# Experts loaded in an order made on the chip, one quad with two blocks of slots per weight load, and residual norms per token tile

## The chip, the cores and the metric

The kernel runs on one core of one Trainium2 chip. The metric is device time in microseconds (us), from one launch to its end. In a core, TensorE (PE in the profile; PEld is its weight load) multiplies, VectorE (DVE), ScalarE (ACT) and GpSimd (POOL) do elementwise work, and SyncE (SP) here only starts transfers. They meet at semaphores. SBUF is the on-chip memory; PSUM, 8 banks of 128 x 512 float32, takes TensorE's results. All data are float32.

## The reference

Two transformer-like blocks on 256 tokens of 1024 channels. The first has attention, a mixture of experts, a pooling mixer, and a second mixture of experts. The second has a mixer, a feed-forward part, another mixer and another feed-forward part, each added to `x` after a norm of its own result:

```python
# first block, each of two layers: the router picks 2 of 32 experts for a token
y = (silu(xb @ w1[e]) * (xb @ w3[e])) @ w2[e]      # w1, w3: 1024 x 512, w2: 512 x 1024
x = x + gate * sum over the token's two experts of weight * y
# second block, each of two layers
x = x + rmsnorm_2(mixer(h), norm_g[layer, 1])
h = rmsnorm_2(x, norm_g[layer, 2])
x = x + rmsnorm_2(swiglu(h, w1, w3, w2), norm_g[layer, 3])   # hidden width 2816
```

With the reference's inputs and its own router, layer 0 sends more than 32 tokens to one expert only (expert 27: 49 tokens), and layer 1 to two (25: 41, 27: 34). Experts 0 to 3 have at most 18 in both layers. No expert has more than 64.

## The kernel before, in words

**Weights and their ring.** All large weights pass through `ring_buffer`, six slots of 2 MB. SP issues the loads in program order. Before it writes a slot it waits on `weights_used`, which PE raises when it has done with a unit; a load raises `weights_landed` of its slot, for which PE waits. A stage's prefetch thus reaches six units ahead and no further.

**Experts** (`experts`, run for layers 0 and 1). Four experts make a quad. Each has 32 slots (`SLOTS`), so a quad fills 128 columns, and each weight matmul is of 32 columns of stationary tokens and 512 columns of moving weights, four side by side. A quad's weights are 12 units, 24 transfers of 1 MB: w1 is units 0 to 3, w3 is 4 to 7, w2 is 8 to 11. PE takes them in six pairs of units. PE's work for quad i (`quad` in `quads_pe`): turn `pick_w`, w1 and w3 by `up` (L1236), `gather` of the next quad's tokens (L1208, a matmul with a 0/1 matrix `pick` that DVE built), turn the product (L1260), w2 (L1269), and `combine` into PSUM banks 0 to 3 (L1279). DVE in step builds the next `pick` (L1326 to L1332) from `dest`, a slot number for each token and choice, less 128 after each quad.

Quads 0 to 7 hold experts 0 to 31 in that order, known when the program is written. An expert's tokens beyond its first 32 go to further blocks of 32 slots in up to four more quads. `table_dve` makes their table on the chip; SP, PE, ACT and DVE each look up in it whether such a quad is live, and SP loads the weights of its live blocks a second time. For a dead quad each engine runs an `Else`: it raises the semaphores that the others expect. There PE and SP go in step: SP (L1172) waits for PE's `weights_used`, then raises the six `weights_landed`, for which PE waits before it raises `weights_used` (L1200) again. A stage barrier, `stage_done`, follows.

**Route.** `route_dve` picks the experts, PE counts (`ranked`), and eleven DVE operations (L1097 to L1110) make `dest`, each waiting for the one before (`Chain`). Then DVE builds `pick`, and PE's first gather starts.

**Residual norms** (`normed_residual`, after `ab_out`, both feed-forward parts and `c_out`). PE multiplies column half by column half for both token tiles of 128 (`project_out`), or row by row of w2 over all four PSUM banks (`feed_forward`, L1593). When all four banks are done, ACT loads the gain row by a transfer of its own, squares the four quarters (L1513), and takes the root (L1516); DVE multiplies by gain and adds to `x` (L1529, L1531). After a barrier the next stage, `norm`, squares `x` (L581), scales it (L604), turns it on PE (L620) into banks 0 to 3, and ACT and DVE copy it to `hT` (L589, L613). After another barrier the matmuls that need `hT` begin. The last residual norm has no `norm` behind it; one transfer of 1 MB writes `x` out (L2322).

## Time and profile before

| What | Value |
|---|---|
| median of 3 runs (lowest, highest) | 2350.74 us (2342.11, 2360.43) |
| the profiled execution, and its span | 2352.67 us, 2350.7 us |
| granted TensorE clock, mean | 0.858 |
| busy: PE / PEld / DVE / ACT / POOL | 1741.1 / 999.5 / 498.7 / 222.3 / 90.2 us |
| transfers of expert weights | 432 of 1 MB |
| layer 0 experts, first gather to last combine | 293 to 795 us |
| layer 1 experts, first gather to last combine | 857 to 1360 us |
| second block | 1385 to 2351 us |

Times in the rows are from the span's start. In a row of the timeline the first number is the start and the second the duration; an entry x128 is 128 instructions in a row. A float32 matmul is recorded as two, so 32 records of L1236 are one pair of units for one block of slots. A row of --windows gives the busy time of each engine in a stretch, then the granted clock of TensorE (1.00 is 2.4 GHz, 0.50 is 1.2 GHz), the share of the DMA engines' time that was busy, and GB/s.

### The profile page before, as it was taken

To read this page: it belongs to the slowest core of one execution; us is meant where nothing else is said; L and a number is where in the kernel's file an instruction comes from. 1 tells how busy PE (TensorE), PEld (TensorE's weight loads), DVE (VectorE), ACT (ScalarE), POOL (GpSimd) and SP (SyncE) were. 2 spreads that over 40 slices of the span, in tenths; PEclk is the share of its full clock that TensorE was granted. 3 is DMA by queue.
4 is the path that set the end of the run, shared out by engine and by line. 5 is a ranking of instruction groups with operands and counts; after the bars stand their busy time and mean duration, and the time that the engine had idled before them with its cause. 6 is when DMAs were issued, how large, how long until landed. Compare 5 with 4: busy or idle time off the path is not lost. (4 is left out here: it accounts for less than half of the span.)

```text
span 2350.7 us, 22507 instructions
## 1 busy us (share of the span) xinstructions
PE 1741.1 (74%) x8954; PEld 999.5 (43%) x8955; DVE 498.7 (21%) x1114; ACT 222.3 (9%) x484; POOL 90.2 (4%) x119
## 2 busy tenths in 40 slices
PE   6999876665666766666666868226999889879997
PEld 3655532222222442222222347113886376548853
DVE  1224331111011243111111132871000023310001
ACT  1011110000000110000000011001000022110000
POOL 1010010000000037000000000000000000000000
PEclk9999987878787777877878887558999989889999
DMA  9968199999999549999999941015334524123230
GB/s 367 376 272 327 72 367 421 422 422 422 422 422 386 192 171 421 422 422 422 422 422 422 399 162 36 0 36 188 122 126 165 183 78 155 59 81 143 108 125 27
DMA packets 128330, 599.76 MB, mean 255 GB/s; under 512 B 14276, under 2 KB 18664, under 8 KB 70536
## 3 DMA queue, kind: packets, MB, share of 16 engines
q1 hardware_dynamic: 122992, 592.78, 63.0%
q10 hardware_dynamic: 4488, 3.78, 0.6%
q0 software_dynamic: 784, 2.26, 0.3%
q8 instruction: 49, 0.80, 0.1%
q14 instruction: 17, 0.14, 0.0%
HBM read 629.19 MB, written 1.05 MB: 268 GB/s over the span
## 5 line engine op out<-in xcount | busy, mean ns | idle before, releaser
L1236 PE MATMUL ps<-ring_buffer,arena 128*32 128x512 f32 x2304 | 347.5, 761 | 230.4 <-DMA ring_buffer<-in_exp_w 227.7
L1582 PE MATMUL ps<-hT,ring_buffer 128*128 128x256 f32 x1408 | 310.9, 384 | 4.5 <-issue 2.6
L1236 PEld LDWEIGHTS ps<-ring_buffer,arena 128*32 128x32 f32 x2304 | 89.6, 135 | 475.6 <-issue 372.3
L1582 PEld LDWEIGHTS ps<-hT,ring_buffer 128*128 128x128 f32 x1408 | 269.9, 192 | 45.5 <-issue 6.3
L1269 PE MATMUL ps<-ring_buffer,arena 128*32 128x512 f32 x1152 | 166.7, 733 | 103.8 <-DMA ring_buffer<-in_exp_w 89.3
L1593 PE MATMUL ps<-ring_buffer,arena 128*128 128x512 f32 x352 | 154.2, 596 | 2.7 <-DVE arena L1612 1.9
L1269 PEld LDWEIGHTS ps<-ring_buffer,arena 128*32 128x32 f32 x1152 | 43.6, 131 | 213.8 <-issue 204.8
L1352 DVE TENSOR_TENSOR arena<-arena,ps 128x512 f32<-128x512 f32 x18 | 19.2, 1065 | 499.8 <-PE ps L1236 499.8
L1593 PEld LDWEIGHTS ps<-ring_buffer,arena 128*128 128x128 f32 x352 | 66.0, 190 | 90.0 <-issue 87.4
L2051 PE MATMUL ps<-hT,ring_buffer 128*128 128x256 f32 x384 | 86.5, 387 | 2.1 <-issue 1.0
L1208 PEld LDWEIGHTS ps<-arena,xn 128*128 128x128 f32 x640 | 77.1, 201 | 24.1 <-issue 15.2
L1208 PE MATMUL ps<-arena,xn 128*128 128x128 f32 x640 | 81.0, 287 | 8.6 <-DVE arena L1327 8.6
L1612 DVE TENSOR_TENSOR arena<-arena,ps 128x256 f32<-128x256 f32 x44 | 18.5, 421 | 298.5 <-ACT arena L1606 298.5
L2051 PEld LDWEIGHTS ps<-hT,ring_buffer 128*128 128x128 f32 x384 | 74.1, 194 | 14.9 <-issue 3.5
L620 PE MATMUL ps<-consts,xn 128*128 128x128 f32 x112 | 22.9, 390 | 75.7 <-DVE xn L604 55.0
L1293 ACT ACTIVATE arena<-ps,mod,gain 128x128 f32<-128x128 f32 x80 | 30.1, 457 | 410.7 <-PE ps L1208 410.7
L1279 PE MATMUL ps<-arena 128*128 128x512 f32 x144 | 66.7, 605 | 0.0
L725 PE MATMUL ps<-hT,ring_buffer 128*128 128x256 f32 x256 | 59.3, 395 | 3.1 <-ACTq L234 2.5
L1305 ACT ACTIVATE arena<-ps 128x512 f32<-128x512 f32 x18 | 10.8, 598 | 527.9 <-PE ps L1236 527.9
L1543 PE MATMUL ps<-ring_buffer,hT 128*128 128x512 f32 x128 | 58.4, 616 | 2.1 <-DVEq L234 1.9
L1362 DVE TENSOR_TENSOR arena<-ps,gates 128x512 f32<-128x512 f32 x18 | 12.5, 692 | 218.5 <-PE ps L1269 218.5
L725 PEld LDWEIGHTS ps<-hT,ring_buffer 128*128 128x128 f32 x256 | 50.5, 199 | 13.1 <-issue 3.3
(442 smaller groups left out, 1522.5 us busy)
## 6 DMA issues: line engine op xcount, KB each, us to landing
ring_buffer<-in_exp_w SPq DMA_DIRECT2D x432, 1024.0 KB
ring_buffer<-in_ffn_w SPq DMA_DIRECT2D x30, 2048.0 KB
ring_buffer<-in_ada_w SPq DMA_DIRECT2D x24, 2048.0 KB
ring_buffer<-in_c_w_in SPq DMA_DIRECT2D x8, 2048.0 KB
ring_buffer<-in_attn_w_in SPq DMA_DIRECT2D x6, 2048.0 KB
ring_buffer<-in_ab_w_in SPq DMA_DIRECT2D x3, 2048.0 KB
ring_buffer<-in_ffn_w SPq DMA_DIRECT2D x6, 1024.0 KB
ring_buffer<-in_attn_w_o SPq DMA_DIRECT2D x2, 2048.0 KB
```

Source lines behind the costliest of these rows:

```text
L620: ins = pe.transpose(ps[:, k // 2, (k % 2) * S + t * P:(k % 2) * S + (t + 1) * P], xn[:, t, k * P:(k + 1) * P], ident)
L725: ins = pe.matmul(ps[:, n % BANKS, 0:S], w[:, k, j * P:(j + 1) * P], hT[:, k, :], start=(k == 0), stop=(k == KD - 1))
L1208: ins = pe.matmul(ps[:, BXA + k // 4, (k % 4) * P:(k % 4 + 1) * P], xn[:, t, k * P:(k + 1) * P], pick[:, t, :], start=(t == 0), stop=(t == ...
L1236: ins = pe.matmul(ps[c, bank, :], xgT[:, 4 * phase + k, c], halves[j][:, k, :], start=(phase == 0 and k == 0), stop=(phase == 1 and k == 3))
L1269: ins = pe.matmul(ps[c, bank, :], prodT[:, 2 * phase + k, c], halves[j][:, k, half * 512:(half + 1) * 512], start=(phase == 0 and k == 0), ...
L1279: ins = pe.matmul(ps[:, 2 * half + t, :], pick_wT[:, t, :], y[:, half * 512:(half + 1) * 512], start=opens, stop=False, skip_group_check=True)
L1293: return eng.activation(o, src, ACT.Identity, scale=G[:, k:k + 1], bias=H[:, k:k + 1])
L1352: dve.tensor_tensor(prod.rearrange("c (h k p) -> c h p k", h=2, k=2), silu_g.rearrange("c (h p k) -> c h p k", h=2, k=2), ps[:, BU, :].rea ...
L1543: ins = pe.matmul(ps[:, 2 * c + t, :], fT[:, k, t * P:(t + 1) * P], w[:, k, :], start=(k == 0), stop=(k == KD - 1))
L1582: ins = pe.matmul(ps[:, f % 8, i * S:(i + 1) * S], w[:, k, j * P:(j + 1) * P], hT[:, k, :], start=(k == 0), stop=(k == KD - 1))
L1593: ins = pe.matmul(ps[:, 2 * half + t, :], aT[:, r + k, t * P:(t + 1) * P], w[:, k, 512 * half:512 * half + 512], start=(r + k == 0), stop= ...
L2051: ins = pe.matmul(ps[:, n % 8, 0:S], w[:, k, j * P:(j + 1) * P], hT[:, k, :], start=(k == 0), stop=(k == KD - 1))
```

## The change

**Order.** Quad 0 keeps experts 0 to 3 and its loads are written out. For the rest DVE makes `order` on the chip: of experts 4 to 31, up to four with over 32 tokens come first and form quad 1 (with the next ones in line, where there are fewer), the others follow. SP waits for `table_ready` after quad 0's loads, and looks up four expert numbers at the head of each of quads 1 to 7. `table_dve` grows from 5 DVE operations to 39 (14 up to `order`); `route_dve` has 5 instead of 11 after `ranked`, which place the tokens of quad 0 alone, and loses 2 of its first ones. `table_dve` still runs after the first gather.

**The wide quad.** Quad 1 is done by `wide_quad`, written out: each weight pair multiplies a block A of 32 slots an expert, and then a block B with slots 33 to 64, and only B's use frees the units. One more gather, combine and set of turns are needed, and more buffers and PSUM banks. Quads 2 to 7 are as before. Four further quads remain possible for what is still left over. In an `Else`, SP now raises `weights_used` itself, and PE waits for nothing.

**Residual norms.** The matmuls before a residual norm go tile by tile (in `feed_forward` for the last two of six w2 units, 6 of 22 rows). ACT and DVE then do for tile 0 both the residual norm and the `norm` behind it, up to the scaled `xn`, and the same for tile 1; PE turns tile 0 when its own matmuls are done, and then tile 1, into banks 4 to 7. No barrier stands between the residual norm and `norm` any more. The gain is loaded at the head of an earlier stage (`load_gain`) into `gates`. The output is written in two transfers, one a tile. The final norm's gain moves from ACT's queue to POOL's.

```diff
+WIDE_QUAD = 1
+BLOCKS = QUADS + 1
...
-                v(dve.tensor_scalar(n_more, count, 1.0 / SLOTS, 0.5 / SLOTS - 1.0 / SLOTS - 0.5, ALU.mult, ALU.add))
-                v(dve.tensor_scalar(n_more, n_more, ROUND, None, ALU.add))
-                v(dve.tensor_scalar(n_more, n_more, -ROUND, 0.0, ALU.add, ALU.max))
-                v(dve.tensor_tensor_scan(more_end, ones[:, 0:N_EXPERTS], n_more, 0.0, ALU.mult, ALU.add))
...
-                v(dve.scalar_tensor_tensor(out=beyond, in0=rank, scalar=float(SLOTS),
-                                           in1=more_slot.unsqueeze(1).to_broadcast(wide), op0=ALU.is_ge, op1=ALU.mult))
-                v(dve.tensor_tensor(slot_of, rank, first_slot.unsqueeze(1).to_broadcast(wide), ALU.add))
-                v(dve.tensor_tensor(slot_of, slot_of, beyond, ALU.add))
-                v(dve.tensor_tensor(hot_x, hot, each_choice(slot_of), ALU.mult))
-                v(dve.tensor_reduce(dest, hot_x, AX.X, ALU.add))
+                v(dve.tensor_tensor(hot_x, hot, each_choice(rank), ALU.mult))
+                v(dve.tensor_reduce(rank_of, hot_x, AX.X, ALU.add))
+                v(dve.tensor_scalar(far, rank_of, SLOTS - 0.5, float(2 * N_EXPERTS * P), ALU.is_ge, ALU.mult))
+                v(dve.scalar_tensor_tensor(out=dest, in0=chosen_f, scalar=float(SLOTS), in1=rank_of, op0=ALU.mult, op1=ALU.add))
+                v(dve.tensor_tensor(dest, dest, far, ALU.add))
...
             def table_dve(dve):
...
+                v(dve.tensor_scalar(later, iota_e, QUAD - 0.5, None, ALU.is_ge))
+                v(dve.scalar_tensor_tensor(out=over, in0=count, scalar=SLOTS + 0.5, in1=later, op0=ALU.is_ge, op1=ALU.mult))
+                v(dve.tensor_tensor_scan(so_far, ones[:, 0:N_EXPERTS], over, 0.0, ALU.mult, ALU.add))
+                v(dve.scalar_tensor_tensor(out=wide, in0=so_far, scalar=QUAD + 0.5, in1=over, op0=ALU.is_lt, op1=ALU.mult))
...
+                shape = [P, N_EXPERTS, N_EXPERTS]
+                v(dve.tensor_tensor(placed, iota_e.unsqueeze(2).to_broadcast(shape), place.unsqueeze(1).to_broadcast(shape),
+                                    ALU.is_equal))
+                v(dve.tensor_tensor(placed, placed, iota_e.unsqueeze(1).to_broadcast(shape), ALU.mult))
+                v(dve.tensor_reduce(order_f, placed, AX.X, ALU.add))
+                dve.tensor_copy(order, order_f).then_inc(table_ready, 1)
...
+                v(dve.tensor_tensor(hot_x, hot, each_choice(slot_of), ALU.mult))
+                v(dve.tensor_reduce(dest, hot_x, AX.X, ALU.add))
...
                 dve.tensor_scalar(table[:, 1, :], block_expert, float(N_EXPERTS), None, ALU.is_lt).then_inc(table_ready, 1)
...
-                with sp.Fori(0, FIRST_QUADS) as i:
+                for u in range(UNITS):
+                    for j in range(2):
+                        load(u, j, 0, 2 * (u % 2) + j)
+                sp.wait_ge(table_ready, 2 * layer + 1)
+                with sp.Fori(1, FIRST_QUADS) as i:
+                    expert = [sp.value_load(order[0:1, bass.ds(QUAD * i + j, 1)], min_val=0, max_val=N_EXPERTS - 1)
+                              for j in range(QUAD)]
                     for u in range(UNITS):
                         for j in range(2):
-                            load(u, j, i, QUAD * i + 2 * (u % 2) + j)
-                sp.wait_ge(table_ready, r0)
+                            load(u, j, i, expert[2 * (u % 2) + j])
...
                             sp.drain().then_inc(weights_landed[slot], 64)
+                        sp.drain().then_inc(weights_used, UNITS)
...
-                        if frees_units:
-                            for slot in range(RING):
-                                eng.wait_ge(weights_landed[slot], base[slot] + 64 + 64 * FIRST_QUADS + 64 * more)
-                            eng.drain().then_inc(weights_used, UNITS)
...
+                def wide_quad(i, b):
+                    pe.wait_ge(weighted, j0 + b + 1)
+                    pe.wait_ge(xa_taken, j0 + b + 1)
+                    turn_weights(BXA)
+                    pe.wait_ge(xb_taken, j0 + b + 1)
+                    pe.wait_ge(yb_taken, j0 + b + 1)
+                    up(i, 0, 0, xgT, BG, g_ready, frees=False)
+                    pe.wait_ge(w_copied, i0 + b + 1)
+                    pe.wait_ge(picked, j0 + b + 2)
+                    gather(pe, False)
+                    pe.wait_ge(ya_taken, j0 + b + 1)
+                    pe.wait_ge(weighted, j0 + b + 2)
+                    turn_weights(BU)
+                    up(i, 0, 1, xgT, BG, g_ready, frees=False)
+                    pe.wait_ge(xa_taken, j0 + b + 2)
+                    up(i, 0, 0, xgT_b, BXA, g_ready)
+                    pe.wait_ge(xb_taken, j0 + b + 2)
+                    up(i, 0, 1, xgT_b, BXA, g_ready)
+                    pe.wait_ge(w_copied, i0 + b + 2)
+                    up(i, 4, 0, xgT, BU, u_ready, frees=False, one=True)
+                    up(i, 4, 1, xgT, BU, u_ready, frees=False)
+                    up(i, 4, 0, xgT_b, BXB, u_ready)
+                    pe.wait_ge(prod_done, i0 + b + 1)
+                    turn_prod(BG)
+                    up(i, 4, 1, xgT_b, BXB, u_ready)
+                    pe.wait_ge(p_copied, i0 + b + 1)
+                    down(i, 0, prodT, (BU, BG), frees=False, one=True)
+                    pe.wait_ge(prod_done, i0 + b + 2)
+                    turn_prod(BXA)
+                    down(i, 1, prodT, (BU, BG), frees=False)
+                    pe.wait_ge(p_copied, i0 + b + 2)
+                    down(i, 0, prodT_b, (BXB, BXA))
+                    down(i, 1, prodT_b, (BXB, BXA))
+                    combine(b, pick_wT, y)
+                    pe.wait_ge(ya_taken, j0 + b + 3)
+                    pe.wait_ge(yb_taken, j0 + b + 3)
+                    pe.wait_ge(picked, j0 + b + 3)
+                    gather(pe, False)
+                    combine(b + 1, pick_wT_b, y_b, frees=False)
...
+                wide_quad(WIDE_QUAD, WIDE_QUAD)
...
+                def wide_quad(b):
+                    dve.wait_ge(combined, j0 + b + 1)
+                    copy_weights(b, pick_wT, BXA)
+                    next_pick(b)
+                    take_half(b + 1, xgT_b)
+                    copy_weights(b + 1, pick_wT_b, BU)
+                    next_pick(b + 1)
+                    multiply(b, silu_g, BU)
+                    copy_prod(b, prodT, BG)
+                    multiply(b + 1, silu_b, BXB)
+                    copy_prod(b + 1, prodT_b, BXA)
+                    take_y(b, y, (BU, BG))
+                    take_y(b + 1, y_b, (BXB, BXA))
+                    take_half(b + 2, xgT)
...
-                    act.dma_start(gates[:, 0, :], A["norm_final_g"].partition_broadcast(P)).then_inc(final_gain_loaded, 16)
...
+                    pool.wait_ge(combined, j0 + 1 + WIDE_QUAD + 2)
+                    pool.dma_start(gates[:, 0, :], A["norm_final_g"].partition_broadcast(P)).then_inc(final_gain_loaded, 16)
...
+            act.dma_start(gates[:, (n + 1) % 2, :], gain_row.partition_broadcast(P)).then_inc(residual_signals[0], 16)
...
+                act.wait_ge(ready, base + 2 * t + 2)
+                for half in range(2):
+                    ins = act.activation(xn[:, t, halves[half]], ps[:, 2 * half + t, :], ACT.Square,
+                                         accum_out=ssq[:, 2 * half + t:2 * half + t + 1])
+                ins.then_inc(summed, 1)
+                act.wait_ge(meaned, at(t))
+                act.activation(rt[:, t:t + 1], ms[:, t:t + 1], ACT.Sqrt).then_inc(rooted, 1)
...
+                act.wait_ge(x_ready, x_at + t)
+                act.activation(xn[:, t, :], x[:, t, :], ACT.Square, accum_out=ssq[:, t:t + 1]).then_inc(summed, 1)
+                act.wait_ge(meaned, at(t) + 1)
+                act.activation(rt[:, t:t + 1], ms[:, t:t + 1], ACT.Sqrt).then_inc(rooted, 1)
+                for k in (2, 3, 6, 7):
+                    act.wait_ge(turned, 2 * (u + t) + k // 4 + 1)
+                    o, i = turned_to(k, t)
+                    act.activation(o, i, ACT.Identity, scale=scale_cols[:, k:k + 1]).then_inc(h_act if t else h_first, 1)
...
+                dve.wait_ge(summed, at(t))
+                m, r = ms[:, t:t + 1], rstd[:, t:t + 1]
+                v(dve.tensor_tensor(m, ssq[:, t:t + 1], ssq[:, 2 + t:3 + t], ALU.add))
+                dve.tensor_scalar(m, m, 1.0 / D, EPS, ALU.mult, ALU.add).then_inc(meaned, 1)
+                dve.wait_ge(rooted, at(t))
+                v(dve.reciprocal(r, rt[:, t:t + 1]))
...
+                for half in range(2):
+                    ins = dve.scalar_tensor_tensor(out=xn[:, t, halves[half]], in0=ps[:, 2 * half + t, :], scalar=r,
+                                                   in1=row_gain[:, halves[half]], op0=ALU.mult, op1=ALU.mult)
+                v(ins)
+                dve.tensor_tensor(x[:, t, :], x[:, t, :], xn[:, t, :], ALU.add).then_inc(x_ready, 1)
...
+                dve.wait_ge(summed, at(t) + 1)
+                dve.tensor_scalar(m, ssq[:, t:t + 1], 1.0 / D, EPS, ALU.mult, ALU.add).then_inc(meaned, 1)
+                dve.wait_ge(rooted, at(t) + 1)
+                v(dve.reciprocal(r, rt[:, t:t + 1]))
+                dve.tensor_scalar(xn[:, t, :], x[:, t, :], r, None, ALU.mult).then_inc(scaled, 1)
+                for k in (0, 1, 4, 5):
+                    dve.wait_ge(turned, 2 * (u + t) + k // 4 + 1)
+                    o, i = turned_to(k, t)
+                    dve.tensor_scalar(o, i, scale_cols[:, k:k + 1], None, ALU.mult).then_inc(h_dve if t else h_first, 1)
...
+                pe.wait_ge(scaled, u + t + 1)
+                if t:
+                    pe.wait_ge(h_first, 8 * n + 8)
+                for k in range(KD):
+                    _, o = turned_to(k, t)
+                    ins = pe.transpose(o, xn[:, t, k * P:(k + 1) * P], ident)
+                    if k % 4 == 3:
+                        ins.then_inc(turned, 1)
...
-                act.dma_start(row_gain, gain_row.partition_broadcast(P)).then_inc(gain_loaded, 16)
...
+                units = [ring.take(pe, (tag, c)) for c in range(2)]
+                for t in range(TT):
+                    for c, w in enumerate(units):
                         for k in range(KD):
                             ins = pe.matmul(ps[:, 2 * c + t, :], fT[:, k, t * P:(t + 1) * P], w[:, k, :],
                                             start=(k == 0), stop=(k == KD - 1))
-                        ins.then_inc(ready, 1)
-                    release(pe)
-            act_, dve_ = normed_residual(ready, 0, gain_row)
+                        ins.then_inc(block_ready, 1)
+                        if t == TT - 1:
+                            release(pe)
+                for t in range(TT):
+                    pe_tile(pe, t)
...
+                units = [(r, n, ring.take(pe, ("w2", r))) for r, n in rows[-2:]]
+                for t in range(TT):
+                    for r, n, w in units:
+                        for k in range(n):
+                            down(w, r, k, t)
+                        if t == TT - 1:
+                            release(pe)
+                for t in range(TT):
+                    pe_tile(pe, t)
...
+            for t in range(TT):
+                sp.wait_ge(x_ready, uses["x"] - TT + t + 1)
+                sp.dma_start(out[0, t * P:(t + 1) * P, :], x[:, t, :]).then_inc(out_written, 16)
+            sp.wait_ge(out_written, 16 * TT)
-            sp.dma_start(out[0].rearrange("(t p) d -> p t d", p=P), x[:, :, :]).then_inc(out_written, 16)
-            sp.wait_ge(out_written, 16)
```

## Rows read from the trace of the kernel before

**Rows 1.** Waits of PE: waiting instruction, releaser: total us, times, longest.
```profile
PE ps L1236 <- DMA ring_buffer<-in_exp_w: 227.7, 53, 6.7
PE ps L1269 <- DMA ring_buffer<-in_exp_w: 89.3, 17, 6.3
```

**Rows 2.** Windows: stretch, length, busy us, granted clock, DMA share, GB/s.
```profile
300.00:305.00 5.00, 5.00 (x48) 1.53 (x52) 4.89 (x5) 1.19 (x1) 4.14 (x2) 1.00 0.16 24
406.00:466.00 60.00, 38.02 (x242) 13.34 (x240) 7.66 (x17) 3.38 (x6) 0.00 (x0) 0.83 1.01 422
764.60:795.00 30.40, 29.20 (x239) 11.76 (x237) 7.47 (x16) 2.10 (x5) 0.00 (x0) 1.00 0.34 114
1329.30:1360.30 31.00, 29.41 (x239) 11.62 (x237) 7.48 (x16) 2.10 (x5) 0.00 (x0) 1.00 0.64 261
794.65:802.98 8.33, 0.00 (x1) 0.00 (x0) 0.00 (x1) 0.00 (x0) 0.00 (x0) 0.70 0.00 0
1360.27:1368.31 8.04, 0.01 (x1) 0.00 (x0) 0.00 (x1) 0.00 (x0) 0.00 (x0) 0.77 0.00 0
```

**Rows 3.** Timeline of PE, layer 0, from quads 0 and 2.
```profile
299.94 10.51 PE L1236 MATMUL ps<-ring_buffer,arena 128*32 128x512 f32 x96 [1.38 <-ACT arena L1293]
...
416.64 6.51 PE L1236 MATMUL ps<-ring_buffer,arena 128*32 128x512 f32 x32 [6.20 <-DMA ring_buffer<-in_exp_w]
426.68 4.92 PE L1236 MATMUL ps<-ring_buffer,arena 128*32 128x512 f32 x32 [3.52 <-DMA ring_buffer<-in_exp_w]
...
441.61 3.84 PE L1208 MATMUL ps<-arena,xn 128*128 128x128 f32 x32
...
461.79 3.71 PE L1279 MATMUL ps<-arena 128*128 128x512 f32 x8
...
466.44 3.64 PE L1236 MATMUL ps<-ring_buffer,arena 128*32 128x512 f32 x32 [0.72 <-DMA ring_buffer<-in_exp_w]
```

**Rows 4.** SP's waits in 672 to 682 us, then in 732 to 742 us.
```profile
SPq L1154 <- PE ps L1236: 7.9, 1, 7.9
...
SPq L1154 <- PE ps L1236: 1.8, 1, 1.8
```

**Rows 5.** Source view of L1200 in 780 to 798 us: PE's first dead quad.
```profile
L1200 PEldq DRAIN  x1: 8/8/8, 796.4 to 796.4; - x1
```

**Rows 6.** Timeline of DVE in layer 1's route and table.
```profile
852.95 0.19 DVE L1097 TENSOR_SCALAR arena<-ps 128x32 f32<-128x32 f32 x1 [1.99 <-PE ps L1041]
...
855.43 0.29 DVE L1110 TENSOR_REDUCE arena<-arena 128x4 f32<-128x128 f32 x1
...
862.97 0.69 DVE L1123 TENSOR_REDUCE arena<-arena 128x16 f32<-128x512 f32 x1
```

**Rows 7.** Timeline of all engines, from ffn0's end to mixer_c's first matmul.
```profile
1872.80 0.60 ACT L1513 ACTIVATE xn<-ps 128x512 f32<-128x512 f32 x1 [78.49 <-PE ps L1593]
...
1875.23 1.28 ACT L1516 ACT_TABLE_LOAD   x1
...
1877.82 0.75 DVE L1529 SCALAR_TENSOR_TENSOR xn<-ps,small,hT 128x512 f32<-128x512 f32 x1 [0.89 <-DMA hT<-in_norm_g]
...
1883.52 1.06 ACT L581 ACTIVATE xn<-x 128x1024 f32<-128x1024 f32 x1 [6.79 <-DVEq L234]
...
1886.45 1.42 DVE L604 TENSOR_SCALAR xn<-x,small 128x1024 f32<-128x1024 f32 x2
...
1888.02 3.65 PE L620 MATMUL ps<-consts,xn 128*128 128x128 f32 x16 [15.69 <-DVE xn L604]
...
1892.62 7.61 PE L2051 MATMUL ps<-hT,ring_buffer 128*128 128x256 f32 x24 [0.96 <-ACTq L234]
```

**Rows 8.** The end: timeline from ffn1's last squares, then the output among DMA issues.
```profile
2336.47 0.60 ACT L1513 ACTIVATE xn<-ps 128x512 f32<-128x512 f32 x1 [78.44 <-PE ps L1593]
...
2346.33 0.39 SPq L2322 DMA_DIRECT2D out<-x  x1
...
out<-x SPq DMA_DIRECT2D x1, 1024.0 KB, 4.0
```

400 lines of the change are left out of this document (236 added, 164 removed).

## The prediction

> **What bounds the kernel now.** I read the page's slices first: in the experts of both layers the DMA engines are full and PE is two thirds busy. The waits of PE say it directly: 227.7 + 89.3 us of waiting for expert weights [rows 1]. So quads 1 to 7 of a layer cost what their weights cost to move: the stretch of 60 us for one quad runs at 422 GB/s with a DMA share of 1.01, and PE has 38 us of work in it, part of it slow, for the granted clock is 0.83 [rows 2]. From one pair of units to the next are 10.0 us [rows 3]. Nothing that leaves these loads in number shortens those quads.
>
> Two kinds of places are not of that kind. First, each layer runs one more quad for overflowing tokens, at the full clock and with a DMA share of 0.34 and 0.64: its few live blocks were loaded ahead, and it is bound by PE, 29.2 of 30.4 us and 29.4 of 31.0 us [rows 2]. Behind it come 8.33 and 8.04 us in which no engine works: three dead quads and the barrier [rows 2]. Second, the second block is bound by PE, and around each residual norm PE waits for a chain of ACT and DVE steps: from 1872.4 (0.4 before the first square) to 1892.6, 20.2 us, of which PE works 3.65 [rows 7]. The joints behind the two mixers run the same instructions, and the last residual norm ends in the output.
>
> **The overflow quad goes.** By the counts in the section on the reference, the overflowing experts (one, then two) are past expert 3 and none is over 64 tokens. So quad 1 holds them all, and no further quad is live. That removes 30.4 + 31.0, less 0.5 because the stretches are cut a little wide: **60.9 us**. The second loading of these experts' weights goes too, but it was hidden.
>
> **What the wide quad costs.** PE's work doubles: twice 29.2 = 58.4 us at full clock, against 60 us of transfer. That it fits is not enough; units are freed later, and a ring that is not freed stops the DMA, which is the bound. I lay it out from the landing of A's first pair at 0; pairs land at 0, 10, ... 50, and pair p+3 needs the slots of pair p when pair p+2 has landed, at 10p + 20. A pair for one block takes 3.64 warm [rows 3], the gather 3.84, combine 3.7.
> A pair 0 to 3.6; gather to 7.5; turn; A pair 1 from 10 to 13.6; B pairs 0 and 1 to 17.3 and 20.9. Pair 0 is free at 17.3, limit 20. A pair 2 to 24.5; idle to 30. After an idle of 3.52 us a pair took 4.92, after 6.20 us 6.51 [rows 3], so A pair 3 takes about 5.7, to 35.7; B pair 2 to 39.3: limit 40. Turn, B pair 3 to 43.3 (limit 50), A pair 4 to 47, turn, A pair 5 from 50 to 55, B pair 4 to about 59 (limit 60), B pair 5 to 62.6. Combine, gather, combine: 74. The next quad's pairs 0 and 1 have landed by 70; PE does them by 82, pair 2 by 86, and has caught up at 90.
> Between a freed slot and data moving there is about 1 us: the first pair's records (a third of 10.51 from 299.94, [rows 3]) end at 303.4, and in 300 to 305 the DMA share is 0.16, that is 0.8 us of 5 [rows 2]. So two limits are missed by 0 to 1 us, and I take 2.5 us a layer, **+5 us**. Bounds: 0, and where PE's work runs at the 0.83 of the neighbouring quads (58.4 / 0.83 = 70.4 us, with some 12 us of waits, 82 us, against 60 and the ring's 10 to 15 us of slack) 10 us a layer. DVE's and ACT's steps (7.66 and 3.38 us a quad, [rows 2], so some 16 and 7 in the wide one) have gaps enough.
>
> **SP's order.** Each of quads 1 to 7 starts with four lookups. Bound from the overflow quad, which did nine (one for live, eight for its table): at the head of quad 7 SP still waited 7.9 us for a free slot, at the head of the overflow quad 1.8 us [rows 4]. So nine cost about 6.1 us, four 2.7 us, out of 7.9 us of slack, and behind them stand two pairs already queued. Cost 0. `order` itself is ready long before: its 14 operations take at most 7 us, and SP asks for it only when quad 0's last unit is issued, which needs PE's sixth unit, some 10 us into quad 0.
>
> **DVE's table.** Eleven chained operations take 2.8 us [rows 6], 0.25 each. The table's 34 new ones: 31 small, 7.8 us, and three of 1024 elements, at most twice the 0.69 of a 512-wide one [rows 6], 4.2 us. They begin about 2 us before quad 0's first matmul and end 11 us into it; the next `pick` is 3.5 us more, 14 us. PE wants it for its gather, not before the fourth pair: 3.5 us to free a slot, 1 to start, 10 to land, 3.6 to use, 18 us. Hidden, by 4 us. In layer 0 POOL runs beside it, and in 300 to 305 DVE had only 5 operations in 4.89 us [rows 2]: up to 4 us late, so at worst +2. I take 0.
>
> **Route.** Before the first gather 11 operations become 5, 2.8 us to about 1.3. The first gather, and with it the first freed slot and everything that the DMA bounds after it, is 1.5 us earlier: **-3 us** for both layers (0 to -3.5).
>
> **Dead quads.** Three become four, but PE and SP no longer go in step. PE's first dead quad, for which SP was ready, ended at 796.4, 1.75 us after the last combine at 794.65 [rows 5]; three took 8.33 with the barrier [rows 2]. Four at 1.7 and 0.4 for the barrier are 7.2: **-2 us** for both. Bounds: four at the old pace of 2.65 are +2.6 a layer; -3 a layer if an iteration is 1.2.
>
> **Residual norms, three with a norm behind.** T is the last matmul. Eight records of a 512-wide matmul take 3.7 us (combine, [rows 3]). Tile 0's matmuls thus end 32 records or 14 us before T in `project_out`, and 24 records or 10.5 us before T in the feed-forward (6 rows, two halves). Its chain: squares 1.3, means 0.4, table and root 1.5, reciprocal 0.2, gain 1.5, add 1.2, square 1.3, root and reciprocal 0.65, scale 0.7 = 8.8 us, done before T. After T: PE turns tile 0, half of 3.65 = 1.8; ACT copies its share by T + 2.8, and only then, its order is fixed, comes to tile 1's squares: 1.3, then 0.4, 0.5, 1.5, 1.2, 1.3, 0.65, 0.7: T + 10.4. Turn 1.8 and last copies and barrier 1.1: T + 13.3. The entries are one tile's share of [rows 7]: a square 0.60, gain 0.75, square of `x` 1.06, scale 1.42 for two, turn 3.65 for both; the table load of 1.28 falls to tile 0. Now it is 20.2; 20.2 - 13.3 = 6.9, and where the gain's transfer lands later than here some tenths more, so 7.3 each, **-22 us** (-15 to -25; not under 5 each, since the gain's transfer and one tile's DVE work, 2.8 us of gain and add, are surely off the path).
> The last norm: now from T = 2336.1 to 2346.3 for the store, 10.2 us [rows 8]; then squares 1.3, 0.4, 0.5, 1.5, 1.2 and 0.1, T + 5.0. And the last transfer is half as long: of 4.0 us [rows 8] about 1.2 us is half of 1 MB at 422 GB/s. **-6 us** (-4 to -7).
> The Trainium skill, "DMA: Bandwidth & Descriptors", section "Anatomy of one DMA", gives 2.0 us plus bytes over 436 GB/s for a transfer from POOL's queue: an estimate by that page of 3.2 us for half the output against 4.4 for the whole, which would make this term the same 1.2 us of gain; the trace has 4.0 for the whole, from SP's queue.
>
> **Sum.** 60.9 - 5 + 3 + 2 + 22 + 6 = 88.9 us off. The profiled execution has a span of 2350.7 us (2352.67 in all); the median of the runs is 2350.74, so the same sum serves: 2350.7 - 88.9 = **2262 us**.
>
> **Rivals.** (a) *The wide quad starves the ring.* Every limit above is met by 3 us or missed by one; the 0.83 of today's quads speaks for it; against it, that the gaps that go with 0.83 nearly vanish there. 10 us a layer instead of 2.5: 2277 us. At its far end all of PE's work in the wide quad is at the low level, 116.8 us against 60 and 15 of slack, 42 us a layer: 2341 us. That end I give 2 in 100; against it stands that the overflow quad, whose work has no gaps either, runs at 1.00 [rows 2]. The Trainium skill, "TensorE: Matmul & The Clock Gate", section "HAM oscillation", says that a burst followed by a wait for the DMA sends the array back to its slow clock, burst after burst; by that rule each of the wide quad's bursts would start slow, which is the far end if no burst lasts long enough. The trace agrees as to the starts behind gaps of 3.52 and 6.20 us [rows 3]; the wide quad has two such gaps, and both are in the sum.
> (b) *The joints keep their length.* Tile 0's turn and copies stand ahead of tile 1's squares on ACT; if waits between engines eat what tiles save, 3 instead of 7.3 each: 2275 us.
> (c) *No quad is skipped*, because an expert overflows that is not in quad 1. The counts speak against it. Then only joints and route gain: +60.9, and the wide quad is paid for: 2323 us.
> (d) *Slower: SP's lookups.* If a lookup on `order` stalled SP past its slack (7.9 us and 20 us of queued pairs), each of 14 quads would stop the DMA. It takes 88.9 / 14 = 6.4 us of stop each, that is about 34 us for four lookups, over ten times the 0.7 of [rows 4]. Then 2351 us and above.
>
> **Numbers.** My forecast 0.70 (2250 to 2270), (a) 0.14 and its far end 0.02, (b) 0.09, (c) 0.03, (d) 0.02. Forecast, (a) and (b) make the range: from 2250 (no starvation, 9 us a joint, quicker dead quads) to 2288 ((a) and half of (b)). Faster by over 1%, that is under 2327 us: 0.95; within 1%: 0.03; slower: 0.02. One per cent is about what a measurement of this kernel can tell from no change.
>
> **What would show it.** Eight gated products a layer from loops and unrolled quads plus one for block B, no quad after quad 7, and 384 expert transfers instead of 432. The DMA share in the wide quad stays at 1.01, or falls to 0.85 and less (rival a). PE idles about 7 us, not 8.3, between last combine and the add. From the last matmul of a joint to the next stage's first, 13.3 us, with the turn of tile 0 right after the matmuls; if ACT's squares of tile 1 start later than T + 3, (b) holds. SP's wait at the head of a quad falls from 7.9 to about 5; near 0, (d). I am wrong at large if PE's pairs in the wide quad take 6 us instead of 3.7, or if joints are bound by something that the trace of before hides.

## The result

| | before | changed |
|---|---|---|
| median (lowest, highest) | 2354.85 us (2342.11, 2360.43) | 2298.44 us (2287.05, 2301.45) |
| ratio to before, 95% interval | | 0.9763 (0.9732, 0.9793) |
| the profiled execution's span | 2350.7 us | 2285.2 us |
| layer 0: first gather to quad 7's last combine; from there to the add | 471.8; 38.2 | 480.2; 10.7 |
| layer 1: the same | 472.4; 38.8 | 490.3; 10.6 |
| the three joints, last matmul to next stage's first | 20.9, 20.3, 21.0 us | 12.0, 12.0, 12.0 us |
| last matmul to the end | 14.7 us | 7.9 us |
| `mixer_c`'s stretch between two joints | 187.0 us | 192.9 us |

The medians are of five executions each. The kernel is faster by 56 us in the medians and by 65.5 in the profiled executions, of which the changed kernel's is the fastest of its five. I had forecast 89. The direction was right, the size was not, and the time lies 10 us above the range. In the rows on layers 0 and 1 the time before holds the overflow quad and three dead quads, that of the changed kernel four dead quads.

Waits of PE in the changed kernel (total us, times, longest); they answer to [rows 1]:
```profile
PE ps L1272 <- DMA ring_buffer<-in_exp_w: 196.1, 47, 7.0
PE ps L1297 <- DMA ring_buffer<-in_exp_w: 90.1, 17, 6.3
...
PE ps L1731 <- DVE xn L1717: 24.2, 3, 8.1
...
PE ps L1245 <- DVE arena L1436: 12.4, 3, 6.9
```
The weights still set the pace. Two waits are new: the turn of tile 1 in the three joints (8.1 us each, planned), and one of the gather's three waits for the pick (6.9 us at once, not planned; the other two, of the first gathers, stood in the kernel before as well). Stretches of the changed kernel: the two wide quads, then last combine to add in both layers, with the columns of [rows 2]:
```profile
348.90:426.30 77.40, 63.62 (x480) 26.01 (x481) 14.40 (x30) 4.20 (x10) 0.00 (x0) 0.89 0.93 380
884.90:972.00 87.10, 65.91 (x480) 26.80 (x482) 30.92 (x31) 4.20 (x10) 18.18 (x5) 0.86 0.83 339
773.81:784.50 10.69, 0.00 (x0) 0.00 (x0) 0.01 (x1) 0.00 (x0) 0.00 (x0) 0.60 0.57 212
1320.61:1331.21 10.60, 0.00 (x0) 0.00 (x0) 0.00 (x0) 0.00 (x0) 0.00 (x0) 0.73 0.54 194
```
In the wide quads the DMA share is 0.93 and 0.83 where an ordinary quad has 1.01, so the transfers, which are the bound, stood still for part of them: 6.2 us in layer 0 (0.08 of 1.01, times 77.40). In layer 1 DVE is busy 30.92 us, twice layer 0's 14.40 for the same 30 or 31 instructions, and POOL is busy too. Both facts are followed up below.

### The profile page after: what moved, and what is told of

It is laid out like the page before. It is cut to its first block and busy times, and to the rows that moved or that the text cites. A ratio compares the mean times of both kernels' runs of the same rounds, so it can differ in the third digit from the quotient of the medians.

```text
span 2285.2 us, 22430 instructions
## 1 busy us (share of the span) xinstructions
PE 1728.7 (76%) x8954; PEld 997.7 (44%) x8955; DVE 522.8 (23%) x1188; ACT 208.2 (9%) x489; POOL 93.5 (4%) x120
## 5 line engine op out<-in xcount | busy, mean ns | idle before, releaser
L1272 PEld LDWEIGHTS ps<-ring_buffer,arena 128*32 128x32 f32 x2048 | 85.0, 136 | 412.6 <-issue 336.2
L1297 PEld LDWEIGHTS ps<-ring_buffer,arena 128*32 128x32 f32 x1088 | 41.0, 130 | 204.9 <-issue 196.7
L2276 PEld LDWEIGHTS ps<-hT,ring_buffer 128*128 128x128 f32 x384 | 73.6, 193 | 14.7 <-issue 3.5
L1311 PE MATMUL ps<-arena 128*128 128x512 f32 x128 | 59.3, 605 | 0.0
```

The costliest lines, as they stand in the source:

```text
L1272: ins = pe.matmul(ps[c, bank, :], tokens[:, 4 * phase + k, c], halves[j][:, k, :], start=(phase == 0 and k == 0), stop=(phase == 1 and k = ...
L1297: ins = pe.matmul(ps[c, bank, :], tokens[:, 2 * phase + k, c], halves[j][:, k, half * 512:(half + 1) * 512], start=(phase == 0 and k == 0) ...
L1311: ins = pe.matmul(ps[:, 2 * half + t, :], weights[:, t, :], values[:, half * 512:(half + 1) * 512], start=opens, stop=False, skip_group_ch ...
L2276: ins = pe.matmul(ps[:, n % 8, 0:S], w[:, k, j * P:(j + 1) * P], hT[:, k, :], start=(k == 0), stop=(k == KD - 1))
```

## The experiments

Two theories came out of the traces. **L**: the wide quad frees its ring slots too late. **O**: in layer 1 DVE builds block B's pick beside POOL's large operations, and the pick comes late. Each has its own experiment, and an unchanged copy ran on the same chip.

**The changed kernel again.** 

> The changed kernel itself, unchanged, as the measure for the three beside it and for how much a profile of it varies. Ratio to before 0.976 (0.973 to 0.980). From the first gather to quad 7's last combine 480 us in layer 0 and 490 us in layer 1, as in its first profile (before: 472 and 472); joints of 12.0 us. Theory O (the pick of block B comes late in layer 1 since DVE works beside POOL's rotation tables): PE again waits about 7 us for the pick and 3 us for the weighted pick in layer 1's wide quad. A rival, that the 18 us of layer 1 are chance, has layer 1 at 480 here.


2295.21 us, ratio 0.976 (0.9736 to 0.9785). 480.4 and 489.5 us; joints 12.0. So layer 1's longer stretch is not chance. Its `mixer_c` was 196.7 us, longer than in the first profile (see further down).

**Theory O.**
```diff
+                if layer:
+                    pool.wait_ge(combined, j0 + 1 + WIDE_QUAD + 2)
                 (s5_tables if layer else pool_weights)(pool)
                 if layer:
-                    pool.wait_ge(combined, j0 + 1 + WIDE_QUAD + 2)
```


> POOL builds the rotation tables (s5_tables) only when the wide quad of layer 1 has been combined, so that nothing large runs on POOL beside the wide quad's picks. Theory O: DVE's pick steps there take 0.9 us again and not 4 to 8; layer 1 from first gather to quad 7's last combine falls from 490 to about 480 us, layer 0 stays at 480; the whole 10 us less than the unchanged kernel (ratio to it 0.996). Rival L alone (all of the wide quad's price is late freed slots): PE's wait for the pick is taken up by the ring, layer 1 stays at 488 to 490 and the time at that of the unchanged kernel.


2284.28 us, 10.9 less than the unchanged copy; layer 1 480.2 us, layer 0 480.3. Theory O holds, and its price is the 9.3 us by which layer 1 fell. It is one profile, but the nine profiles in which the wide quad and the tables are as in the changed kernel have 487.4 to 490.5 us. Timelines of the changed kernel around layer 1's wide quad, PE, then DVE, then POOL (start us, duration):
```profile
884.86 3.64 PE L1272 MATMUL ps<-ring_buffer,arena 128*32 128x512 f32 x32 [0.83 <-DMA ring_buffer<-in_exp_w]
895.42 5.41 PE L1245 MATMUL ps<-arena,xn 128*128 128x128 f32 x32 [6.92 <-DVE arena L1436]
904.28 0.41 PE L1283 MATMUL ps<-consts,arena 128*128 128x128 f32 x2 [3.45 <-DVE arena L1441]
```
```profile
884.48 1.93 DVE L1459 TENSOR_SCALAR arena<-arena 128x4 f32<-128x4 f32 x1
886.45 5.08 DVE L1435 TENSOR_TENSOR arena<-consts,arena 128x256 f32<-128x256 f32 x2
891.56 3.71 DVE L1436 TENSOR_TENSOR arena<-arena 128x256 f32<-128x256 f32 x1
895.20 8.47 DVE L1440 TENSOR_TENSOR arena<-arena 128x256 f32<-128x256 f32 x2
```
```profile
882.77 3.61 POOL L461 TENSOR_TENSOR arena<-arena 128x2048 f32<-128x2048 f32 x1
886.46 4.78 POOL L462 TENSOR_TENSOR arena<-arena,hT 128x2048 f32<-128x2048 f32 x1
891.33 3.67 POOL L463 TENSOR_TENSOR hT<-arena 128x2048 f32<-128x2048 f32 x1
895.07 3.67 POOL L464 TENSOR_TENSOR arena<-arena 128x2048 f32<-128x2048 f32 x1
898.82 4.57 POOL L465 TENSOR_TENSOR arena<-arena,hT 128x2048 f32<-128x2048 f32 x1
```
And DVE with the tables later:
```profile
886.59 0.16 DVE L1459 TENSOR_SCALAR arena<-arena 128x4 f32<-128x4 f32 x1
886.79 0.89 DVE L1435 TENSOR_TENSOR arena<-consts,arena 128x256 f32<-128x256 f32 x2
887.71 0.43 DVE L1436 TENSOR_TENSOR arena<-arena 128x256 f32<-128x256 f32 x1
888.05 0.88 DVE L1440 TENSOR_TENSOR arena<-arena 128x256 f32<-128x256 f32 x2
```
Look at where each slow DVE entry ends (start plus duration): L1459 at 886.41, L1435 at 891.53, L1436 at 895.27, L1440 at 903.67. POOL's instructions end at 886.38, 891.24, 895.00 and 903.39, each 0.03 to 0.29 us earlier. So DVE's steps wait until a POOL instruction is over. For the three entries with two inputs in SBUF, L1435, L1436 and L1440, that is what the Trainium skill, "SBUF — State Buffer", section "Who interferes with whom", states of DVE instructions with two inputs in SBUF beside a GpSimd one that reads SBUF: they share a read interface, and whoever comes second is blocked for the other's whole instruction. The trace agrees, with 0.43 against 3.71 us for L1436. L1459 has one input in SBUF, so that rule on two inputs does not speak of it; the trace shows its wait all the same.

**Theory L, by taking work away.** 

> Block B of the wide quad multiplies only a quarter of the up products and half of the down products (k = 3 alone, k = 1 alone); the rest of its products is left out, all loads, waits and other steps stay. Theory L (the wide quad frees its slots too late for the ring; a slot refilled lands 13 to 14 us after it is freed, 3 more than a pair's 10): with about 18 us less of PE's work slots are freed in time, layer 0 falls from 480 to 472 or 474 us and layer 1 from 490 to 476 to 482 (the late pick stays). Rival, that the 8 us in layer 0 are lookups of SP or the steps of DVE and not the held slots: layer 0 stays at 478 to 480.


This kernel leaves out part of block B's products, so its result is not the program's. Layer 0 474.6, layer 1 483.1 us; 2286.64 us in all. Layer 0 lost 5.8 of its 8.6 us and layer 1 6.4, so they end 0.6 and 1.1 us above what was expected. The stretch of its wide quad in layer 0:
```profile
351.00:425.00 74.00, 54.28 (x362) 22.61 (x364) 15.33 (x34) 4.21 (x10) 0.00 (x0) 0.86 0.99 405
```
The held slots are the main part, and SP's lookups or DVE's steps, which are all still there, are not. The granted clock is 0.86 here, no better than the 0.89 of the changed kernel, and the DMA share is back at 0.99: slots that come free early are enough, at a slow clock too.

**Theory L, by order alone.**
```diff
-                    up(i, 0, 1, xgT, BG, g_ready, frees=False)
                     pe.wait_ge(xa_taken, j0 + b + 2)
                     up(i, 0, 0, xgT_b, BXA, g_ready)
+                    up(i, 0, 1, xgT, BG, g_ready, frees=False)
...
-                    up(i, 4, 1, xgT, BU, u_ready, frees=False)
                     up(i, 4, 0, xgT_b, BXB, u_ready)
+                    up(i, 4, 1, xgT, BU, u_ready, frees=False)
...
-                    down(i, 1, prodT, (BU, BG), frees=False)
                     pe.wait_ge(p_copied, i0 + b + 2)
                     down(i, 0, prodT_b, (BXB, BXA))
+                    down(i, 1, prodT, (BU, BG), frees=False)
```


> The same work in another order on PE: block B's product on pair 0 before A's on pair 1, B's on pair 2 before A's on pair 3, B's on pair 4 before A's on pair 5. PE does them while it would wait for the next landing, and pairs 0, 2 and 4 are freed 4 to 12 us earlier. Theory L: layer 0 falls from 480 to 473 or 475 us, layer 1 from 490 to 480 to 484; the whole 10 to 15 us less than the unchanged kernel (ratio 0.994 to 0.996). Rival P (PE has too much work in the wide quad, whatever the order): both stay, ratio to the unchanged kernel 0.999 to 1.001.


2281.02 us, ratio to before 0.9696 (0.9673 to 0.972), 14.2 us less than the unchanged copy. Layer 0 471.4 us, which is what it was before the change (471.8); layer 1 483.2. Rival P falls: the same products fit, in another order. PE's timeline in layer 0's wide quad of the changed kernel:
```profile
348.93 3.64 PE L1272 MATMUL ps<-ring_buffer,arena 128*32 128x512 f32 x32 [0.78 <-DMA ring_buffer<-in_exp_w]
...
358.88 5.34 PE L1272 MATMUL ps<-ring_buffer,arena 128*32 128x512 f32 x32 [2.32 <-DMA ring_buffer<-in_exp_w]
364.00 7.08 PE L1272 MATMUL ps<-ring_buffer,gates 128*32 128x512 f32 x64
...
380.16 5.21 PE L1272 MATMUL ps<-ring_buffer,arena 128*32 128x512 f32 x32 [5.64 <-DMA ring_buffer<-in_exp_w]
385.18 3.62 PE L1272 MATMUL ps<-ring_buffer,gates 128*32 128x512 f32 x32
...
402.77 12.71 PE L1297 MATMUL ps<-ring_buffer,arena 128*32 128x512 f32 x96 [5.79 <-DMA ring_buffer<-in_exp_w]
```
Block B's products read `gates`. B is done with pair 0 half way through the 64 records from 364.00, at 367.6, and pair 3, which takes those slots, is used from 380.16: 12.6 us. B is done with pair 2 at 388.80, and pair 5 is used from 402.77: 14.0 us. A pair takes 10.0 [rows 3], so 2.6 and 4.0 us pass besides. From A's first pair on the landings come at 31.2 and 53.8 instead of 30 and 50. Where the time goes shows in the changed kernel's stretches of 1 us around the first of these slots, and at the end of the wide quad:
```profile
365.00:366.00 1.00, 1.00 (x16) 0.34 (x11) 0.00 (x0) 0.00 (x0) 0.00 (x0) 1.00 0.96 401
366.00:367.00 1.00, 1.00 (x12) 0.31 (x8) 0.00 (x0) 0.00 (x0) 0.00 (x0) 1.00 0.26 107
367.00:368.00 1.00, 1.00 (x16) 0.45 (x12) 0.00 (x0) 0.00 (x0) 0.00 (x0) 1.00 0.10 41
368.00:369.00 1.00, 1.00 (x16) 0.34 (x11) 0.00 (x0) 0.00 (x0) 0.00 (x0) 1.00 0.42 66
369.00:370.00 1.00, 1.00 (x12) 0.31 (x8) 0.00 (x0) 0.00 (x0) 0.00 (x0) 1.00 0.75 238
...
412.00:413.00 1.00, 1.00 (x16) 0.27 (x8) 0.00 (x0) 0.00 (x0) 0.00 (x0) 1.00 0.00 0
413.00:414.00 1.00, 1.00 (x12) 0.27 (x8) 0.17 (x1) 0.00 (x0) 0.00 (x0) 1.00 0.88 164
```
The last two columns are the DMA share and GB/s. The last transfer of pair 2 lands at 368.7, but the share falls from 366.0 on, to 0.26 and 0.10: nearly all of the data had moved 2.7 us before the landing, and nothing was queued behind them. SP issues the next transfer at 367.67, right after the slot is free, and its first packets start at 368.7. So from a freed slot to moving data it is about 1 us, as the prediction says; what comes too early is the end of the queued data. Such holes come three times in this wide quad: 2.5 us here, 0.9 around 390, and 2.9 around 412, where pair 4's slots are free only at 412.0, 63.1 us after A's first use. In the reordered kernel:
```profile
347.73 3.64 PE L1272 MATMUL ps<-ring_buffer,arena 128*32 128x512 f32 x32 [0.47 <-DMA ring_buffer<-in_exp_w]
...
355.28 3.64 PE L1272 MATMUL ps<-ring_buffer,gates 128*32 128x512 f32 x32
...
377.55 3.64 PE L1272 MATMUL ps<-ring_buffer,arena 128*32 128x512 f32 x32 [2.86 <-DMA ring_buffer<-in_exp_w]
...
397.44 7.08 PE L1297 MATMUL ps<-ring_buffer,arena 128*32 128x512 f32 x64 [1.30 <-DMA ring_buffer<-in_exp_w]
```
Pair 0 is free 11.2 us after A's first use and not 18.7, and the landings come at 29.8 and 49.7. The stretch of its wide quad:
```profile
348.50:416.00 67.50, 58.66 (x480) 24.46 (x476) 14.35 (x31) 4.21 (x10) 0.00 (x0) 1.00 1.01 420
```
The DMA share is back at 1.01, and with PE's gaps at 2.86 us and less the granted clock is 1.00 and not 0.89. This run thus mends both the late slots and the slow products, and does not by itself tell them apart; the run with fewer products, at a clock of 0.86, does so in part.

**Each half of the change alone.** 

> The kernel before with the experts' part of the change alone (order, wide quad, route); joints and output as before. By the terms as measured: overflow quads -60.9, wide quads +8 and +17, eight dead quads +5, route -3: -34 us against before (ratio 0.9855). Theory J (the changed joints are followed by some 9 us more in mixer_c, where the granted clock falls longer): mixer_c's stretch here is 187 us as before. Rival C (that clock is chance from run to run, in either kernel): it is 187 in some profiles and 193 to 197 in others, whatever the joints.


2314.03 us, ratio 0.9838 (0.9804 to 0.9872), that is 37 us less; `mixer_c` 188.8.

> The kernel before with the residual norms, gain loads and output of the change alone; the experts as before. Joints 12.0 us each instead of 20.2 to 21.0 (-26) and -7 at the end: -33 us. Theory J: mixer_c 193 to 197 us instead of 187, so the whole is -23 to -27 (ratio 0.989 to 0.990). Rival C: -33 us (ratio 0.986), or anything between from run to run.


2324.80 us, ratio 0.9885 (0.9848 to 0.9922), that is 26 to 27 less, theory J's sum; but rival C's ratio of 0.986 lies inside the interval too, so the time alone does not choose between them. Joints 12.0 us, `mixer_c` 192.8: the stretch is what speaks for J.

**Dead quads.** 

> The changed kernel without its loop over quads for further blocks (four iterations a layer, all dead here; such quads would be left out where tokens need them). From the last combine to the add 0.3 to 1 us instead of 10.7 us in each layer, if PE's own way through four dead iterations is all that stands there: 20 us less than the changed kernel (ratio to before 0.967). Rival: DVE's or ACT's way through their four iterations or SP's is what the barrier waits for; gone as well here, same 20 us. If less than 15 us go, the barrier waited for something else.


2269.03 us, ratio 0.9639 (0.9607 to 0.9672); 0.1 us from last combine to add in both layers, 10.6 and 10.5 less. The median is 26 us below that of the unchanged copy, which ran on another chip; the stretches explain 21 of it, and what the other 5 are no run shows. The source view of the loop's head in the changed kernel, 773 to 785 us:
```profile
L1229 DVEq ALU_OP  x4: 40/40/40, 773.0 to 779.4; - x4
...
L1229 PEldq ALU_OP  x4: 36/36/36, 776.9 to 784.2; - x4
```
Three steps from 776.9 to 784.2 are 2.43 us a dead quad for PE, and the first ends 3.1 us after the last combine at 773.8. DVE is done at 779.4, and SP issues the next stage's transfers from 777.5 on; both are ahead of PE. So no handshake with SP sets the pace: PE's own lookup, branches and nine signals do.

**The second look at `mixer_c`.** 

> The kernel before once more, for a second profile of it. Theory J: mixer_c 187 us again. Rival C: 187 to 197. From layer 0's last add to layer 1's first gather 54 us again, or, if that is chance of the clock too (five profiles of the changed kernel and its relatives have 45.9 to 52.6), anything from 47 to 56.


2344.82 us; `mixer_c` 184.8, and 47.4 us from layer 0's add to layer 1's first gather. The 54.2 us of the first profile were at the long end: this stretch has 47.4 to 54.2 in three profiles of the kernel before and 45.8 to 53.0 in those of the changed one and its relatives.

> The kernel before, a third profile. If the longer mixer_c belongs to the short joints, its stretch here is 185 to 189 us, with 17 to 24 us of slow clock in it; if it was chance, 190 to 200 can come here too.

> The experts' part alone with the old joints, a second profile. As above: mixer_c 185 to 189 us if it belongs to the short joints, anything up to 200 if chance.

> The joints alone, a second profile: mixer_c 192 to 197 us if it belongs to the short joints, anything from 185 if chance.


186.9, 188.8 and 196.9 us. Five profiles with the old joints have 184.8 to 188.8, and all nine with the new ones and no padding 192.8 to 196.9. It belongs to the joints. Then their length was put back, behind `ffn0` alone:
```diff
+                if n == 1 and t == 1:
+                    for _ in range(3):
+                        v(dve.tensor_scalar(xn[:, t, :], x[:, t, :], r, None, ALU.mult))
                 dve.tensor_scalar(xn[:, t, :], x[:, t, :], r, None, ALU.mult).then_inc(scaled, 1)
```


> The changed kernel with DVE's scaling of tile 1 done three times more (same values) in the residual norm behind ffn0: that joint some 2.3 us longer, 14.3 instead of 12.0 us. Mixer_c's stretch behind it was 185 to 189 us in three profiles with the old joints and 193 to 197 in seven with the new. Theory J1 (where TensorE's clock falls inside mixer_c depends on where the joint ends against the clock's own rhythm, so it can be moved): mixer_c leaves 193 to 197 and gets to 185 to 189 with at least one of the three pads. Rival J2 (a joint under some length between 12 and 20 us leads to it): 193 to 197 for the short pads, 185 to 189 for the longest alone. Rival J3 (it is the order of work or the gain's transfer, not the length): 193 to 197 for all three.

> The same with six scalings more: the joint some 4.6 us longer, 16.6 us. Mixer_c: by J1 either, by J2 193 to 197 or, if the length that counts is shorter, 185 to 189; by J3 193 to 197.

> The same with eleven scalings more: the joint some 8.4 us longer, 20.4 us, as long as the old joint. By J1 either, most likely 185 to 189 since the old joints were as long; by J2 185 to 189 us; by J3 193 to 197 us.

> The changed kernel with the joint behind ffn0 padded to the old length, a second profile: 191 us again if mixer_c follows from where the joint ends, 185 to 189 if the joint's length decides, anything if chance.


Joints of 14.3, 16.7 and twice 20.65 us gave `mixer_c` stretches of 200.4, 195.3 and twice 191.1 us. Most of the difference (all but at most 2.5 us) lies in one part of `mixer_c`, from its first transpose to the first matmul of `c_out`: small matmuls with gaps between. That part in five kernels: before, the experts alone, the changed kernel again, then padded by 3 and by 11:
```profile
2011.49:2049.11 37.62, 29.64 (x193) 21.94 (x193) 20.09 (x56) 8.89 (x42) 0.00 (x0) 0.84 0.12 45
```
```profile
1967.29:2009.15 41.86, 33.91 (x192) 24.95 (x193) 20.11 (x56) 8.89 (x42) 0.00 (x0) 0.77 0.11 43
```
```profile
1957.74:2006.29 48.55, 40.62 (x192) 29.72 (x192) 20.12 (x56) 8.88 (x42) 0.00 (x0) 0.62 0.10 37
```
```profile
1958.75:2009.90 51.15, 43.25 (x192) 31.11 (x192) 20.11 (x56) 8.88 (x42) 0.00 (x0) 0.55 0.09 34
```
```profile
1964.34:2006.19 41.85, 33.90 (x192) 24.99 (x192) 20.10 (x56) 8.90 (x42) 0.00 (x0) 0.77 0.11 42
```
DVE and ACT do the same in all (20.1 and 8.9 us); PE's 192 or 193 records take 29.6 to 43.3 us, and the granted clock falls from 0.84 to 0.55 in step. So the time goes to a slower TensorE clock, and how long it stays slow changes with the joint ahead: the joint of 20.65 us has the same 41.85 us as the experts-alone kernel with its joint of 20.1. Rival C (chance) falls, since repeats agree within 0.1 us or fall on one of few values (44.3 and 48.6 for the same kernel), and those with old and new joints do not overlap. J3 (order or the gain's transfer, 193 to 197 for every pad) falls with the shortest pad's 200.4 and the longest's 191.1. J1 and J2 did not come out as written either: no pad got to 185 to 189, and the way is no straight one, for 14.3 us gave the worst. Nor does the joint's length alone set the time: the kernel before has 37.6 us behind joints of 20.2 to 20.3, and one joint of 12.0 goes with 44.3 or 48.6. Which rule sets it stays open. Padding by 8.7 us brings back 2 to 6, so it costs more than it gains.

**All remedies.** The reordered wide quad, the tables later, and one look at the first further quad:
```diff
+                any_live = eng.value_load(quad_live[0:1, 0:1], min_val=0, max_val=1)
+                with eng.If(any_live > 0):
...
+                with eng.Else():
+                    for s in signals:
+                        eng.drain().then_inc(s, QUADS - FIRST_QUADS)
```


> Three remedies at once on the changed kernel: the reordered wide quad, POOL's rotation tables behind layer 1's wide quad, and one look at the first further quad in place of four (where it is dead the rest are too, and every semaphore is raised at once by the sum of the four). By the single runs: layer 0 from first gather to quad 7's last combine 471 us (as before the change), layer 1 472 us if the two causes are all there was (476 if something third is left), from last combine to add 2 to 3.5 us instead of 10.7. So -9, -18 and -15: about 2253 us (ratio to before 0.957 to 0.961).


2259.11 us, ratio to before 0.9598 (0.957 to 0.9627): some 36 us less than the unchanged copy (by the medians; the chips differ, and by the ratios to before it is 38), and better than both kernels. 471.3 and 473.4 us for the experts, so the two causes are nearly all that there was; 5.2 and 2.7 us behind them, of which the 5.2 is more than expected, and 6 us of the sum to 2253 are missing.

## Why the forecast was wrong

| Term | forecast | measured |
|---|---|---|
| overflow quads gone | -60.9 | -29.9 and -30.8 |
| wide quads | +5 | +8.4 and +17.9 |
| route | -3 | -1.6 in each layer, by profiles |
| dead quads | -2 | +2.4 and +2.6 |
| joints | -22 | -26.2 |
| last norm and output | -6 | -6.8 |
| `ffn0`, `mixer_c` | 0 | +2, +6 to +10 |

With 8 for `mixer_c` (the means over all profiles with new and old joints, 195.4 and 187.3) and 3 for the route these make -55; the medians have -56. The upper end of the range was mis-added, too: (a) and half of (b) are 2277 + 6.5 = 2284 and not 2288; 2298 lies above either.

**The mechanism held.** The overflow quad is gone: 384 expert transfers instead of 432, no quad behind quad 7, 61 us. SP's lookups and DVE's table cost nothing that shows: rival (d) is out, for SP's longest wait around the head of a quad was 4.6 us, as "about 5" said. In layer 0 two steps of the table took 3.29 and 2.21 us beside POOL, and the pick behind it was ready 3.5 us before PE's gather. Rival (c) is out as well.

**The step that failed first** is the limit that the wide quad was measured by: "pair p+3 needs the slots of pair p when pair p+2 has landed, at 10p + 20". By then most of the DMA engines have been idle for 2.7 us. To prevent that a slot must be free about 1 us before the queued data end, which is some 3.7 us before that landing and not 1. The working's limits of 20, 40 and 60 us for pairs 0, 2 and 4 become some 16, 36 and 56; its own layout had them free at 17.3, 39.3 and 59, so all three were missed in it, and they were free at 18.7, 39.9 and 63.1. The step beside it, "Between a freed slot and data moving there is about 1 us", came out right (1.0 us). What is lost in the holes isn't caught up, since the DMA is the bound: 6.2 of the 8.4 us. Where the other 2 are no run shows.

Rival (a), the starved ring, had the right effect and about the right size, 10 us a layer. Its cause was given as slow products, and that is a part only: with B's products thinned out the clock stayed at 0.86, and still 5.8 us came back. In the changed kernel three slow bursts (5.34, 5.21 and 5.84 us for a pair) stand behind gaps of 2.32, 5.64 and 5.79 us, and the first of them, for which the working had 3.6, made pair 0 free 1.7 us later. The Trainium skill, "TensorE: Matmul & The Clock Gate", section "HAM oscillation", has that pattern; the trace agrees for these bursts, and no farther: the burst behind 0.78 us took 3.64, and so did one behind 2.86 us in the reordered kernel.

**The second** is "DVE's and ACT's steps have gaps enough". By their sum they have. But the wide quad needs block B's pick 3.6 us after its start, where quads 2 to 7 need it 26 to 36 us after; and POOL's tables run just then in layer 1. Before, the same steps took 3.7 to 4.8 us a line in layer 1's quad 1, and were hidden. I had counted POOL's interference only for the table in layer 0. Price: 9.3 us.

**The third** is the pace of dead quads. "Ended 1.75 us after the last combine" [rows 5] was read as the price of an iteration. It was that of one whose lookup PE had made ahead (between 794 and 803 us the trace has only two lookups for the three), and the others took 3.1 us before and 2.43 now. Four of them cost more than three, so the sign was wrong, by the bound that I had named (+2.6 a layer) and not taken.

**The joints were right**, and better by 1.3 us each. Timeline of the changed kernel, from `ffn0`'s end to `mixer_c`'s first matmul; it answers to [rows 7]:
```profile
1825.84 1.09 PE L1731 MATMUL ps<-consts,xn 128*128 128x128 f32 x8
1826.53 1.14 ACT L1694 ACTIVATE hT<-ps,cols 128x128 f32<-128x128 f32 x4 [4.12 <-PE ps L1731]
...
1827.54 0.61 ACT L1680 ACTIVATE xn<-ps 128x512 f32<-128x512 f32 x1
...
1829.67 1.41 DVE L1707 SCALAR_TENSOR_TENSOR xn<-ps,small,gates 128x512 f32<-128x512 f32 x2
1831.12 1.22 DVE L1710 TENSOR_TENSOR x<-x,xn 128x1024 f32<-128x1024 f32 x1
1832.38 1.06 ACT L1688 ACTIVATE xn<-x 128x1024 f32<-128x1024 f32 x1 [2.93 <-DVE x L1710]
...
1834.99 1.97 PE L1731 MATMUL ps<-consts,xn 128*128 128x128 f32 x8 [8.06 <-DVE xn L1717]
...
1837.71 2.50 PE L2276 MATMUL ps<-hT,ring_buffer 128*128 128x256 f32 x5 [0.75 <-DVEq L236]
```
Matmuls end at 1825.7. Tile 0's turn takes 1.09 us at the fast clock and not the 1.8 of [rows 7], so tile 1's squares start at T + 1.8 and not T + 2.8. Rival (b) is out. The end of the kernel was as worked out: T + 4.85 to the store for 5.0.

**What no step had** is the stretch behind a joint. The sum took "the next stage" as fixed, and 8 of the 26 us that the joints won were given back through the clock in `mixer_c`, 2 more in `ffn0`, where no run looks for the cause.

The profiled execution was 11 us better than the median. Across its stretches the layer 0 add to layer 1's first gather was at the short end (45.9 us of 45.8 to 54.2), and `mixer_c` had the shorter of its two lengths (192.9).

## What to carry to other kernels

When a weight buffer is held longer, count its limit from the end of the queued data and not from their landing (here most data had moved 2.7 us before it, and from a freed slot to moving data is 1 us more), and let the use that frees a slot go ahead of a product on data that hasn't landed. When work is moved, ask when each small input is now needed, and what runs beside its producer at that moment; gaps in an engine's sum say nothing of it. A loop iteration that does nothing still costs its lookup, branches and signals on the slowest sequencer, so one test for all stands better than four.

## What was not expected of the hardware

One 128x256 addition of two SBUF operands on DVE took 3.71 us beside POOL's 128x2048 operations and 0.43 without; even a 128x4 subtraction took 1.93 instead of 0.16. Stretches with the same instructions on PE (the part of `mixer_c`) took 37.6, 41.9, 44.3, 46.1, 48.6 or 51.2 us, with the granted clock between 0.84 and 0.55; the four of these that were repeated (all but 46.1 and 51.2) agree to 0.1 us. They change with the joint 120 us earlier, but one joint of 12.0 us has gone with 44.3 and with 48.6. When a transfer into the ring landed at 368.7, with none queued behind it, the DMA share had been at 0.26 and then 0.10 in the two us from 366.0 to 368.0. A dead loop iteration on PE takes 2.43 us, and on DVE about 2.1 (773.0 to 779.4 in three steps).
